# First modulation in pairs of pieces, and two output chunks of the attention that give their slots back early

## What is computed

```
mod = silu(c) @ ada_w + ada_b               # 1024 x 6144: six rows of 1024
sh1, sc1, g1, sh2, sc2, g2 = split(mod, 6)
u    = rms_norm(x, mix_pre_g) * (1 + sc1) + sh1
proj = u @ w_in                             # queries, keys, values, gates, gated conv
...                                         # convolutions, mLSTM, w_out, FFN
# second block, layer 0: attention with forget gates, 16 heads
out = softmax(q k^T + decays) v
h   = h + rmsnorm(out @ w_out, gain)        # then FFN, a recurrent layer, FFN
```

## Time and profile before

| | us |
|---|---|
| median of 3 runs (lowest to highest) | 2236.34 (2234.01 to 2236.71) |
| the profiled execution | 2233.94 |
| its span, first to last instruction | 2231.9 |
| TensorE busy | 2179.8 (98% of the span) |
| VectorE busy | 1116.3 (50%) |
| GpSimd busy | 1497.8 (67%) |
| ScalarE busy | 664.0 (30%) |
| mean traffic of DRAM | 97 GB/s |

### The profile page before, as it was taken

The page is one execution under the profiler, slowest core; times in us unless marked ns, Lnnn a source line. Parts: engine busy times, 40 slices in busy tenths (PEclk is TensorE's granted clock), DMA queues, the critical chain, the costliest instruction groups (busy, mean ns, idle before and its releaser), DMA issues.

```text
span 2231.9 us, 26833 instructions
## 1 busy us (share of the span) xinstructions
PE 2179.8 (98%) x9588; PEld 1707.0 (76%) x9588; DVE 1116.3 (50%) x1982; ACT 664.0 (30%) x1142; POOL 1497.8 (67%) x741
## 2 busy tenths in 40 slices
PE   7999999999999999999999999999999999999997
PEld 3877777868888887788867888886787777888885
DVE  6889984984333104777643222105877835222102
ACT  3413335122222103444442111104555534111100
POOL 5868675757777887645379777886333258777785
PEclk9999999999999999999999999999999999999999
DMA  6323223633323332222123333332222122333332
GB/s 248 101 84 95 78 83 122 250 128 103 94 91 92 99 104 85 86 76 76 48 95 95 94 94 94 99 103 81 65 67 67 58 69 82 94 94 94 94 104 85
DMA packets 56371, 215.98 MB, mean 97 GB/s; under 512 B 6216, under 2 KB 6216, under 8 KB 53088
## 3 DMA queue, kind: packets, MB, share of 16 engines
q1 hardware_dynamic: 52992, 206.96, 28.8%
q10 hardware_dynamic: 3296, 7.91, 1.0%
HBM read 212.70 MB, written 2.15 MB: 96 GB/s over the span
## 4 chain that ended last, share of the span: by engine, by line
PE 76%; DVE 11%; POOL 5%; issue 3%; ACT 2%; DMA 2%; SPq 0%; DVEq 0%; POOLq 0%; ACTq 0%
PE ps L370 60%; DVE y L2035 5%; PE ps L602 2%; POOL w_lo L979 2%; POOL w_hi L973 2%; DMA raw<-in_wstream 2%; PE ps L407 2%; PE ps L1283 1%; PE ps L393 1%; PE ps L1191 1%; PE ps L394 1%; PE ps L397 1%; DVE qk L2046 1%; PE ps L1314 1%; PE ps L1420 1%
## 5 line engine op out<-in xcount | busy, mean ns | idle before, releaser
L979 POOL TENSOR_TENSOR w_lo<-raw,w_hi 128x1024 fp32r<-128x1024 f32 x335 | 815.5, 2434 | 200.3 <-ACT w_hi L1878 176.4
L973 POOL TENSOR_TENSOR w_hi<-raw,ones 128x1024 fp32r<-128x1024 f32 x304 | 580.7, 1910 | 402.9 <-DMA raw<-in_wstream 402.4
L370 PE MATMUL ps<-u_hi,w_hi 128*128 128x512 f32 x1760 | 715.8, 407 | 6.1 <-DVE qk L2046 2.4
L370 PE MATMUL ps<-u_lo,w_hi 128*128 128x512 f32 x1760 | 695.5, 395 | 0.0
L370 PE MATMUL ps<-u_hi,w_lo 128*128 128x512 f32 x1760 | 695.1, 395 | 0.0
L370 PEld LDWEIGHTS ps<-u_hi,w_hi 128*128 128x128 f32 x1760 | 331.4, 188 | 85.9 <-issue 6.2
L370 PEld LDWEIGHTS ps<-u_hi,w_lo 128*128 128x128 f32 x1760 | 330.2, 188 | 80.5
L370 PEld LDWEIGHTS ps<-u_lo,w_hi 128*128 128x128 f32 x1760 | 331.0, 188 | 75.7 <-issue 3.6
L370 PE MATMUL ps<-f_hi,w_hi 128*128 128x512 f32 x528 | 208.6, 395 | 0.0
L370 PE MATMUL ps<-f_lo,w_hi 128*128 128x512 f32 x528 | 208.6, 395 | 0.0
L370 PE MATMUL ps<-f_hi,w_lo 128*128 128x512 f32 x528 | 208.5, 395 | 0.0
(11 more groups left out here) (366 smaller groups left out, 2905.5 us busy)
## 6 DMA issues: line engine op xcount, KB each, us to landing
raw<-in_wstream SPq DMA_DIRECT2D x342, 512.0 KB, 3.6
ada_buf<-in_ada SPq DMA_DIRECT2D x16, 1024.0 KB, 6.1
ada_start<-in_ada SPq DMA_DIRECT2D x8, 1024.0 KB, 16.8
cbc<-decay_rows ACTq DMA_DIRECT2D x7, 512.0 KB, 3.7
x<-in_xT SPq DMA_DIRECT2D x1, 2048.0 KB, 8.2
bc<-gate_rows ACTq DMA_DIRECT2D x4, 512.0 KB, 5.3
out_T<-x ACTq DMA_DIRECT2D x8, 256.0 KB, 2.2
prm<-in_params SPq DMA_DIRECT2D x1, 357.5 KB, 3.0
```

The lines of the kernel that those rows point to most:

```text
L370: last = nc.tensor.matmul(out, a, b, start=(start and k == 0 and i == 0), stop=(stop and k == nk - 1 and i == 2))
L973: g.tensor_tensor(w_hi[slot][:], raw[slot][:], ones[:, 0:1].to_broadcast([P, D]), ALU.mult).then_inc(chunk_hi, 1)
L979: g.tensor_tensor(w_lo[slot][:], raw[slot][:], w_hi[slot][:].bitcast(f32), ALU.subtract).then_inc(chunk_split, 1)
```

## The change

**The first modulation.** Pieces are loaded and used in four pairs: the scale piece 4 + p and the shift piece p give the column factors of tiles 2p and 2p + 1. All scale pieces go to DVE (`ada_scale_dve`, the same eight operations) and TensorE's sum over partitions; all shift pieces go to TensorE, now with the 128x128 block of the piece as the stationary operand and the column of silu(c) as the moving one (16 matmuls of one column for each piece), so that the result is a column at once and ACT has no part in it. SyncE loads `x` in two halves, and the first three weight chunks between the pieces of the first pairs. TensorE does, in this order: shift 0, sum 0, the mean of the squares, shift 1, sum 1; tiles 0 and 1 times the first two chunks; shift 2, sum 2; tiles 2 and 3 times the first two chunks; shift 3, sum 3; tiles 0 to 3 times the third chunk; tiles 4 to 7 times all three. The matmuls of no use are gone.

**The attention's output.** `kept` holds the last rows of two chunks (four ACT copies), the second chunk's slot is given back after its k = 6 step, and the first output tile's reader waits for one chunk more.

```diff
-    def ada_start_pe(pe, p):
-        ...
-            last = nc.tensor.matmul(ps[(0, 1, 2, 4)[i]][0:1, 0:ADA_COLS], cvec[:, k:k + 1],
-                                    ada_start[:, p, k, :], start=(k == 0), stop=(k == KT - 1))
+    def ada_scale_dve(dve, pair):
+        piece = ada_start[:, ADA_PAIRS + pair]
+        part = ps[1][:, pair % 2 * ADA_COLS:(pair % 2 + 1) * ADA_COLS]
+        dve.wait_ge(ada_start_landed[ADA_PAIRS + pair], 16)
+        ...
+    def ada_columns_dve(dve, pair):
+        dve.wait_ge(p_ada0.sem, p_ada0.at(f"sums{pair}"))
+        ...
+    def ada_shift_pe(pe, pair):
+        pe.wait_ge(ada_start_landed[pair], 16)
+        if pair:
+            pe.wait_ge(v_ada0.sem, v_ada0.at(f"mod{pair - 1}"))
+        for h in range(ADA_COLS // P):
+            j = pair * (ADA_COLS // P) + h
+            for k in range(KT):
+                nc.tensor.matmul(ps[2][:, j:j + 1], ada_start[:, pair, k, h * P:(h + 1) * P], cvec[:, k:k + 1],
+                                 start=(k == 0), stop=(k == KT - 1))
+    def first_tiles_dve(dve, N, pair):
+        ...
@@ SyncE
-        sp_.dma_start(x[:], xT).then_inc(x_landed, 16)
+        sp_.dma_start(x[:, 0:KT // 2, :], xT[:, 0:KT // 2, :]).then_inc(x_landed, 16)
+        sp_.dma_start(x[:, KT // 2:KT, :], xT[:, KT // 2:KT, :]).then_inc(x_rest_landed, 16)
+        load_first(ADA_PAIRS)
+        load_first(0)
+        load_chunk(0, 0, wait=False, at_=places[0])
+        load_first(ADA_PAIRS + 1)
+        load_chunk(1, 1, wait=False, at_=places[1])
+        load_first(1)
+        load_chunk(2, 2, wait=False, at_=places[2])
+        for pair in (2, 3):
+            load_first(ADA_PAIRS + pair)
+            load_first(pair)
@@ TensorE
-        keep_busy(pe, 2, 5)
-        gemm_pair_first(pe, 0, ...)
+        ada_shift_pe(pe, 0)
+        ada_scale_sums_pe(pe, 0)
+        pe.wait_ge(q_n0.sem, q_n0.at(f"sq{KT - 1}"))
         N0.pe2.did(nc.tensor.matmul(ps[7][:], mean_w[:], acc[:], start=True, stop=True), "sum")
+        ada_shift_pe(pe, 1)
+        ada_scale_sums_pe(pe, 1)
+        first_pair_pe(0, range(GROUP - 1))
+        ada_shift_pe(pe, 2)
+        ada_scale_sums_pe(pe, 2)
+        first_pair_pe(1, range(GROUP - 1))
+        ada_shift_pe(pe, 3)
+        ada_scale_sums_pe(pe, 3)
+        for pair in range(2):
+            first_pair_pe(pair, range(GROUP - 1, GROUP))
+        for pair in range(2, 4):
+            first_pair_pe(pair, range(GROUP))
@@ VectorE
+        ada_scale_dve(dve, 0)
+        ada_scale_dve(dve, 1)
+        ada_columns_dve(dve, 0)
+        ...
+        first_tiles_dve(dve, norms[0], 0)
+        ada_columns_dve(dve, 1)
+        ada_scale_dve(dve, 2)
+        first_tiles_dve(dve, norms[0], 1)
+        ada_columns_dve(dve, 2)
+        ada_scale_dve(dve, 3)
+        first_tiles_dve(dve, norms[0], 2)
+        ada_columns_dve(dve, 3)
+        first_tiles_dve(dve, norms[0], 3)
@@ attention output
-                if self.kept and (n, k) == (0, KT - 2):
+                if self.kept and n < len(self.kept[2]) and k == KT - 2:
-            weights[0] = self.kept[2]
+            weights[:len(self.kept[2])] = self.kept[2]
-        out_act(act, outs[2], C_FOXOUT, (KT,), (0, 1, 2, 4, 5), lambda n: C_FOXOUT + max(n + 1, 2))
+        out_act(act, outs[2], C_FOXOUT, (KT,), (0, 1, 2, 4, 5), lambda n: C_FOXOUT + max(n + 1, 3))
```

More of the change, by code:

```diff
@@ L230, in build @@
     pr = [place(f"pr{i}", T) for i in range(2)]
+    last_row = place("last_row", 4 * P, f32r, [2, 2, P])
     assert here[0] <= mix_end
@@ L486, in norm_act @@
                     act.wait_ge(x_landed, 16)
+                elif n == KT // 2:
+                    act.wait_ge(x_rest_landed, 16)
                 if n >= 2 and N.post:
@@ L635, in finish @@
                 last = nc.tensor.matmul(self.out(n), wh, self.lo(k), start=False, stop=True)
-                if n or not self.kept:
+                if not self.kept or n >= len(self.kept[2]):
                     last.then_inc(gemm_done, 1)
@@ L742, in ada_start_act @@
[L742 to L756, removed]
+    def ada_scale_dve(dve, pair):
[3 more added lines that the diff above has]
+        for k in range(KT):
+            if k == 0:
+                ins = nc.vector.tensor_scalar(part, piece[:, 0, :], cvec[:, 0:1], None, ALU.mult)
+            else:
+                dve.wait_ge(v_ada0.sem, v_ada0.at(f"l{pair}_{k - 1}"))
+                ins = nc.vector.scalar_tensor_tensor(part if k < KT - 1 else ada_acc0[:, pair, :], piece[:, k, :],
+                                                     cvec[:, k:k + 1], part, ALU.mult, ALU.add)
+            v_ada0.did(ins, f"l{pair}_{k}")
@@ new lines, in first_tiles_dve @@
+    def first_tiles_dve(dve, N, pair):
+        tiles = (2 * pair, 2 * pair + 1)
+        for n in tiles:
+            if n >= 2:
+                dve.wait_ge(N.vl.sem, N.vl.at("lo", n - 2))
+            N.vt.did(nc.vector.scalar_tensor_tensor(ps[(6, 3)[n % 2]][:], x[:, n, :], col_a[:, n:n + 1], ps[7][:],
+                                                    ALU.mult, ALU.mult), "t")
+        for n in tiles:
+            dve.wait_ge(N.ah.sem, N.ah.at("hi", n))
+            N.vl.did(nc.vector.scalar_tensor_tensor(u_lo[:, n, :], ps[(6, 3)[n % 2]][:], mod[:, n:n + 1],
+                                                    u_hi[:, n, :].bitcast(f32), ALU.add, ALU.subtract), "lo")
@@ L1344, in _ @@
         fox_out = MixerOut(outs[2], C_FOXOUT, lambda k: a_hi[:, k, :], lambda k: a_lo[:, k, :], a_fox, v_fox,
-                           banks=(0, 1, 2, 4, 5), width=4, kept=(a_fg, "last_row", [last_row[:, j, :] for j in range(2)]),
+                           banks=(0, 1, 2, 4, 5), width=4, kept=(a_fg, "last_row", [[last_row[:, n, j, :] for j in range(2)] for n in range(2)]),
                            free=((v_qlow, "ql", PAIRS - 1), (v_qlow, "kl", PAIRS - 1), (a_proj, "v", PAIRS - 1),
@@ L1788, in _ @@
                 if i + 1 == PAIRS and n == 0:
-                    act.wait_ge(chunk_split, C_FOXOUT + 1)
-                    for j, w in enumerate((w_hi, w_lo)):
-                        ins = A(last_row[:, j, :], w[C_FOXOUT % SLOTS][:, (KT - 1) * P:KT * P].bitcast(f32), ACT.Identity)
+                    act.wait_ge(chunk_split, C_FOXOUT + 2)
+                    for c in range(2):
+                        for j, w in enumerate((w_hi, w_lo)):
+                            ins = A(last_row[:, c, j, :], w[(C_FOXOUT + c) % SLOTS][:, (KT - 1) * P:KT * P].bitcast(f32), ACT.Identity)
                     a_fg.did(ins, "last_row")
```

98 lines of the change are left out of this document (39 added, 59 removed).

## The result

| | before | after |
|---|---|---|
| median, us (20 runs each on one chip) | 2235.77 | 2238.71 |
| lowest to highest, us | 2232.49 to 2238.69 | 2231.37 to 2240.62 |
| ratio to before, 95% interval | | 1.0013 (1.0007 to 1.0019) |
| the profiled execution, us | 2233.94 | 2238.02 |
| its span, us | 2231.9 | 2236.2 |

The change costs 2.9 us, which is within 0.2%: no difference by the bound of the prediction. The forecast was +6.0 us. The time lies in the stated range of 2230 to 2250 us, but that range was wide enough to hold "no change" too, and the likeliest outcome ("slower") did not come.

A forecast was written before the change was run, and what follows sets the result against it. TensorE, busy 98% of the span, was taken as the bound: a 41 us start plus a dense stream. +7.4 (first group) +2.7 (mixer) -4.1 (attention's output) = +6.0 us, median 2242.3, range 2230 to 2250.

The forecast's parts named there:

- the likeliest outcome ("slower"): Whole kernel: a median above 2240.8 us, given a chance of 0.60.
- first group's end: TensorE's start: the first 72 products end at 65.7 us instead of 58.3, 7.4 us later.
- mixer behind it: Mixer: VectorE's convolution chain starts 4.9 us later against TensorE; after its waiting, 2.7 us more remain (bounds 0 to 4.7).
- attention's output: Attention's output: TensorE's 2.56 us wait for the sixth chunk and the 1.55 us clock loss behind it go, -4.1 us.
- The clock: Modulation: one-column matmuls neither raise nor hold TensorE's clock; 32 take 7.0 us at the lower level, 3.75 at the upper.
- Rival B: Modulation: clock is low but loads don't slow; group ends 59.1, in all -0.6 us, 2235.7; chance 0.20.
- rival A: Modulation: one-column matmuls hold or raise the clock; third chunk's first dozen ends 43.8, in all -7.5 us, 2228.8; chance 0.10.
- the doubling: TensorE's small matmuls take twice as long at the lower clock: 1.22 us against 0.61 for a group of four.
- Rival C: First group: twelve products are too few to raise the clock; end 71.7, in all +12.0 us, 2248.3; chance 0.15.
- VectorE's last slack: Mixer: VectorE's remaining 2.0 us of waiting at 134.61 us, taken to absorb part of its lag.
- Rival D: Attention's output: the second chunk's slot isn't free earlier; in all +10.1 us, 2246.4; chance 0.07.

The follow-up runs named there:

- e_rows2: Changed kernel with shift pieces streamed as rows into the third chunk's output bank, copied by ScalarE, VectorE's sums still in PSUM: 2235.8 us, 1.0002 to before.
- e_best2: `e_rows2` with the third chunk's last twelve products last and VectorE's scale pieces 2 and 3 one place earlier: 2229.76 us, 0.9976; again 2229.36, 0.9974.
- the second profile: The changed kernel run and profiled again with no edit: 2236.45 us, 1.0009 to the kernel before.
- e_third: Changed kernel with the last twelve products of the first group's third chunk behind those of chunks 0 and 1: 2236.13 us, 1.0009 to the kernel before.
- e_mod: Changed kernel with the attention part undone, so the modulation part alone: 2241.96 us, 1.0030 to the kernel before.
- e_fill: Changed kernel with eight useless streamed matmuls of 256 columns inside each shift piece: 2251.69 us, 1.0074 to the kernel before.

## Why the prediction was right or wrong

| step | forecast, us | in the trace, us |
|---|---|---|
| first group's end | +7.4 (65.7) | +6.4 (64.7) |
| mixer behind it | +2.7 | +1.1 |
| attention's output | -4.1 | -4.3 |
| sum | +6.0 | +3.2 |
| chance fall at 352 us | none | +1.55 |

**The clock: right, with one thing swapped.** 32 one-column records took 6.96 and 6.83 us at the lower level (forecast 7.0), and the clock fell behind both later pieces. Rival B needed 3.8 us at the lower level and rival A a clock that stays up: both fall by the L737 rows. They were needed for that: the four matmuls of the earlier trace rows, from which I took the doubling, stream 128 columns each, so they could not show by themselves that a load slows. Rival A's end, 52.2 us, was also too early, as it left VectorE out: with the clock up nearly throughout, `e_rows2` and `e_best2` ended the group at 60.0 and 57.7. Rival C needed the products not to raise the clock; they did, at 36.4 us, within one dozen. But I had let the clock fall inside a shift piece (4.6 us) and rise inside a dozen of products (4.8). It fell just behind the piece (3.8) and rose at the dozen's end (5.2): for a piece, its sums and a dozen together 9.8 us (36.40 to 46.19) against 10.1 (37.0 to 47.1). In the second profile they changed inside a piece (4.87 us) and inside a dozen (4.2 us), as forecast, so that detail is chance. The end came out 1.0 us early, and that much was there before the first product, which started at 31.22 instead of 32.2: the first piece landed 0.3 us earlier than my estimate, and each one-column record cost 0.21 rather than 0.22, 0.2 and 0.3 us on the two pieces.

**The mixer: the step that failed.** I priced it as VectorE's lag, 4.9 us less its 2.0 us of waiting, and held that TensorE's own stall at the fourth chunk, about 1 us, lay inside. The stall was right: 1.08 us, and `e_third` takes it away. The lag was not there. ACT and its queue before:

```profile
69.70 0.69 ACT L1508 ACTIVATE qk<-ps,prm 128x512 f32<-128x512 f32 x1 [4.60 <-PE ps L370]
69.72 0.53 ACTq L1573 DMA_DIRECT2D gate_rows<-rA  x1
...
73.77 0.40 ACTq L1490 DMA_DIRECT2D bc<-gate_rows  x1
```

and after:

```profile
77.26 0.69 ACT L1544 ACTIVATE qk<-ps,prm 128x512 f32<-128x512 f32 x1 [1.14 <-PE ps L371]
...
79.38 0.52 ACTq L1609 DMA_DIRECT2D gate_rows<-rA  x1
...
81.45 0.40 ACTq L1526 DMA_DIRECT2D bc<-gate_rows  x1
```

ACT stood 4.60 us for TensorE in front of the gate rows and now stands 1.14. The gates' chain does not hang on VectorE's order alone, as I had written: ACT's place in it waits for TensorE, and that wait took in most of the lag. `bc` is issued 7.7 us later than before, against a group 6.4 us later: 1.3 relative to it, not 4.7. At the place of VectorE's last slack the kernel after has

```profile
131.70 0.69 DVE L2067 TENSOR_TENSOR ps<-ps,sg 128x512 f32<-128x512 f32 x1
...
141.80 1.68 DVE L2098 SCALAR_TENSOR_TENSOR sp<-ps,wt 128x512 f32<-128x512 f32 x4
```

7.19 us later than 134.61 and with no wait: the 2.01 us are used up, as forecast, but 7.19 is less than TensorE's own 7.55, so TensorE does not wait for it. My lower bound for this term was 0, from "some slack hidden"; the slack was in a row of ACT that I had not read.

**The attention: right in wait and size; the clock's share is in part luck.** -2.8 us for the wait and -1.5 for the clock against the first profile of the kernel before, and by the ratios 3.1 and 3.6. The 1.55 us of the clock were forecast as certain; `e_mod` waited at the same place and lost nothing. Rival D falls.

**The sum** is +3.2 without the chance fall, against a measured 2.9 (0.0007 to 0.0019 of 2236 is 1.6 to 4.2 us). The profiled pair differs by 4.1 us, mostly because one had the fall at 352 us and the other had not: a comparison of two single profiles is open by about 1.5 us for each such place, and there are at least three: near 352, near 902, and behind the wait for the sixth chunk.

## What to carry to other kernels

Ask of each matmul that a change puts on TensorE not only its length but its kind: blocks of 128 x 128 with a single moving column are work that keeps the engine busy and loses the clock for the products behind it, so the price is theirs. When a lag is carried forward through a pipeline, walk every engine on the chain and look for its own waits: the slack of the engine between two others (ACT's 4.60 us here) hides as much as that of the last. And before a difference between two single profiles is explained, take a second profile of the same kernel.

## What the runs showed of the hardware that I had not expected

- One-column matmuls mixed with streamed ones (`e_fill`) kept the clock at 1.00 for 7 us at a time, but did not raise it in 13.7 us of the same mixture.
- The clock fell behind the same wait of TensorE (2.4 to 2.7 us, at about 352 us of the kernel before) in eight of the thirteen profiles of this study and not in the other five. Near 902 us it fell in six of the thirteen. Each fall cost 1.4 to 1.8 us. Behind the wait of 2.4 to 2.6 us for the sixth chunk it fell in two of the three profiles that have this wait. Waits of 1.8 us in `e_best2` cost no fall.
- A chain of VectorE operations from SBUF to SBUF ran at 1.5 to 2.4 us an operation beside GpSimd, three to five times its 0.5 us; the same chain through PSUM was not slowed.
